# First block of a decoder step: GpSimd's remainders in groups behind DVE's scalings, the memory rows counted by tile, the norm weight spread by TensorE

## The reference

```python
mem_n = rmsnorm(mem_prompt, g_mem[l])                 # 256 memory rows of 1024
mk = mem_n @ w_ck[l];  mv = mem_n @ w_cv[l]           # their keys and values
...
z = rmsnorm(x, g_mix) @ w_in                          # zq, zf, zi, zg, zu, zv, 512 columns each
q = silu(zq); f = lb + (1 - lb) * sigmoid(zf); k = (1 - lb) * sigmoid(-zf); v = zi
S_new, o = hgrn2_scan(S0, q, k, log(f), v)            # recurrence over the tokens, by chunks
o_hg = rmsnorm(o) * hg_norm_g * sigmoid(zg)
o_cm = gelu(zu) * (tril(W_s) @ layernorm(gelu(zv)) + b_s)
x = x + concat(o_hg, o_cm) @ w_out
```

## Time and profile before

| what | us |
|---|---|
| median of 3 runs (2933.69 to 2934.37) | 2933.81 |
| the profiled execution | 2933.21 |
| its span in the trace | 2931.4 |
| PE busy | 2886.1 (98%) |
| DVE busy | 1251.3 (43%) |
| ACT busy | 642.9 (22%) |
| POOL busy | 440.9 (15%) |

### The profile page before, as it was taken

How to read it: one execution, slowest core, us unless ns; L and a number is a source line. 1 busy time by engine, 2 the same in 40 slices (tenths; PEclk the granted TensorE clock), 3 DMA queues, 4 the chain that set the end, 5 groups by cost and what they waited for, 6 DMA issues and landing times.

```text
span 2931.4 us, 40394 instructions
## 1 busy us (share of the span) xinstructions
PE 2886.1 (98%) x17243; PEld 2334.1 (80%) x17243; DVE 1251.3 (43%) x2096; ACT 642.9 (22%) x999; POOL 440.9 (15%) x362
## 2 busy tenths in 40 slices
PE   8998999999999999999999999999999999999998
PEld 7787787777888888788788888877778888877787
DVE  5578443453344733322243744222234473322233
ACT  4435221110123411111122422101012341211011
POOL 0182408788810000000000000000000000000000
PEclk9999999999999999999999999999999999999999
DMA  8895757989975455665666445566767545567654
GB/s 311 311 324 187 278 188 279 361 288 310 329 255 174 154 185 204 222 231 199 223 215 223 142 176 185 199 250 250 274 236 273 178 155 187 180 226 286 235 193 150
DMA packets 207677, 675.93 MB, mean 231 GB/s; under 512 B 22864, under 2 KB 28240, under 8 KB 207504
## 3 DMA queue, kind: packets, MB, share of 16 engines
q1 hardware_dynamic: 200480, 662.72, 63.3%
q10 hardware_dynamic: 7024, 10.68, 1.0%
HBM read 542.84 MB, written 130.48 MB: 230 GB/s over the span
## 4 chain that ended last, share of the span: by engine, by line
PE 89%; DVE 6%; SPq 1%; DMA 1%; ACT 1%; issue 0%; POOL 0%; ACTq 0%; DVEq 0%
PE half L946 81%; PE half L954 2%; PE half L1275 2%; DVE lvl L2238 1%; PE half L1087 1%; PE half L963 1%; DVE lvl L2251 1%; PE half L1155 1%; DMA w_raw<-in_w_out 0%; PE half L1285 0%; DMA mem_raw<-in_w_ck 0%; SPq L599 0%; DMA w_pairs<-stage 0%; DVE state L2287 0%; SPq L779 0%
## 5 line engine op out<-in xcount | busy, mean ns | idle before, releaser
L946 PE MATMUL half<-a_hi,w_ring 128*128 128x512 f32 x2560 | 822.6, 397 | 0.0
L946 PE MATMUL half<-w_ring,a_hi 128*128 128x512 f32 x2176 | 677.1, 392 | 0.0
L946 PE MATMUL half<-w_ring,ht_hi 128*128 128x512 f32 x2016 | 626.5, 392 | 0.0
L946 PEld LDWEIGHTS half<-a_hi,w_ring 128*128 128x128 f32 x2560 | 480.2, 188 | 131.6 <-issue 14.3
L946 PE MATMUL half<-a_lo,w_ring 128*128 128x512 f32 x1280 | 505.4, 395 | 0.0
L946 PEld LDWEIGHTS half<-w_ring,a_hi 128*128 128x128 f32 x2176 | 410.3, 189 | 90.0
L946 PEld LDWEIGHTS half<-w_ring,ht_hi 128*128 128x128 f32 x2016 | 378.9, 188 | 82.2
L946 PE MATMUL half<-w_ring,a_lo 128*128 128x512 f32 x1088 | 433.6, 399 | 5.1 <-DVE a_lo L1839 3.6
L946 PE MATMUL half<-w_ring,ht_lo 128*128 128x512 f32 x1008 | 395.5, 392 | 0.8 <-DVE ht_lo L2464 0.8
L2472 DVE SCALAR_TENSOR_TENSOR x<-half,rstd,x 128x512 f32<-128x512 f32 x252 | 171.7, 744 | 300.7 <-PE half L946 300.7
L946 PEld LDWEIGHTS half<-a_lo,w_ring 128*128 128x128 f32 x1280 | 240.2, 188 | 56.2
(11 more groups left out here) (309 smaller groups left out, 2473.6 us busy)
## 6 DMA issues: line engine op xcount, KB each, us to landing
w_ring<-w_pairs SPq DMA_DIRECT2D x704, 512.0 KB, 3.2
w_pairs<-w_ring SPq DMA_DIRECT2D x192, 512.0 KB, 5.0
w_pairs<-stage SPq DMA_DIRECT2D x16, 1024.0 KB, 6.0
w_raw<-in_w_up SPq DMA_DIRECT2D x64, 256.0 KB, 4.5
w_raw<-in_w_down SPq DMA_DIRECT2D x64, 256.0 KB, 3.9
w_s<-in_w_up SPq DMA_DIRECT2D x8, 2048.0 KB, 11.1
w_s<-in_w_down SPq DMA_DIRECT2D x8, 2048.0 KB, 11.5
w_raw<-in_w_in SPq DMA_DIRECT2D x48, 256.0 KB, 4.3
```

What stands on the lines that cost most here:

```text
L946: m = nc.tensor.matmul(ps[:, j, :], l, r, start=(i == 0 and q == 0), stop=(i == tiles_in - 1 and q == 2))
```

## The change

- `FILLER_HI` has other places for the casts: 33 to 36 behind `kt`, 37 to 39 in unit 0, 40 to 43 in unit 1, 44 and 45 in unit 2, 46 to 48 in unit 3, 49 to 51 in unit 4, 52 to 54 in unit 5, 55 in unit 6.
- GpSimd waits, before the remainders of tiles 29, 33, 37, 40, 44, 46, 49 and 52, for the scalings of units 0 to 7.
- The memory rows come in two loads with a semaphore each; ACT and DVE wait for them by tile.
- The norm weight comes as one row of 4 KB; PE spreads it into PSUM with two products of `ident`'s first element by 512 columns, and DVE's scaling reads it from there.
- Eight products of zeros stand ahead of that, ten more behind the transposes of the rows.
- The gelu table is loaded behind unit 5's `rsqrt`, ahead of the casts.

```diff
-WARM = 20
+WARM = (8, 10)
-FILLER_HI = {"zq": range(29, 33), "kt": range(33, 34), 0: range(34, 38), 1: range(38, 42), 2: range(42, 45), 3: range(45, 47), 4: range(47, 48),
-             5: range(48, 52), 6: range(52, 56)}
+FILLER_HI = {"zq": range(29, 33), "kt": range(33, 37), 0: range(37, 40), 1: range(40, 44), 2: range(44, 46), 3: range(46, 49),
+             4: range(49, 52), 5: range(52, 55), 6: range(55, 56)}
+FILLER_TURN = {29: 0, 33: 1, 37: 2, 40: 3, 44: 4, 46: 5, 49: 6, 52: 7}
...
-            for dst, src in ((x[:, 0:MT, :], I["mem_prompt"][0].rearrange("(t p) d -> p t d", p=P)),
-                             (ident[:], I["c_ident"]), (gain[:], I["g_mem"][0:1, :].broadcast_to([P, D]))):
+            for dst, src in ((gain[0:1, :], I["g_mem"][0:1, :]), (ident[:], I["c_ident"])):
                 sp.dma_start(dst, src).then_inc(mem_in, 16)
+            for t in range(MT):
+                sp.dma_start(x[:, t, :], I["mem_prompt"][0, t * P:t * P + P, :]).then_inc(mem_rows_in[t], 16)
...
             for i in range(first, after):
-
+                if i in FILLER_TURN:
+                    pool.wait_ge(scaled_ready.sem, scaled_ready.at("first", FILLER_TURN[i]))
                 pool.wait_ge(filler_hi, i - first + 1)
...
-            for i in range(WARM):
-                nc.tensor.matmul(half[1][:, 3, 0:P], zero[:].to_broadcast([P, P]), zero[:].to_broadcast([P, P]),
-                                 start=True, stop=True)
-            pe.wait_ge(mem_in, 48)
+            zeros(WARM[0])
+            pe.wait_ge(mem_in, 32)
+            for c in range(2):
+                m = nc.tensor.matmul(half[0][:, 2 + c, :], ident[0:1, 0:1].to_broadcast([1, P]),
+                                     gain[0:1, c * 512:c * 512 + 512], start=True, stop=True)
+            m.then_inc(gain_spread, 1)
             for t in range(MT):
                 pe.wait_ge(xn_ready.sem, xn_ready.at(pos, ("nm", t)))
                 transposes(pos, ("nm", t), [xn[:, t, k * P:k * P + P] for k in range(KD)])
+            zeros(WARM[1])
...
-            act.wait_ge(mem_in, 48)
+            act.wait_ge(mem_rows_in[0], 16)
...
                         rsqrt(pos, "oa", 12)
+                        tables("gelu_apprx_tanh_and_others")
                     filler_tiles(u)
...
-            dve.wait_ge(mem_in, 48)
...
+            dve.wait_ge(gain_spread, 1)
             for t in range(MT):
-                nc.vector.tensor_tensor(xn[:, t, :], x[:, t, :], gain[:], ALU.mult).then_inc(xn_ready.sem, 1)
+                dve.wait_ge(mem_rows_in[t], 16)
+                nc.vector.tensor_tensor(xn[:, t, :].rearrange("p (a c) -> p a c", a=2),
+                                        x[:, t, :].rearrange("p (a c) -> p a c", a=2), half[0][:, 2:4, :], ALU.mult
+                                        ).then_inc(xn_ready.sem, 1)
```

More of the change, by code:

```diff
@@ L378, in program @@
         h0, h1, tl, dn = zip(*(jobs.counts[p] for p in phases))
-        mem_in, consts_in = sem("mem_in"), sem("consts_in")
+        mem_in, consts_in, gain_spread = sem("mem_in"), sem("consts_in"), sem("gain_spread")
+        mem_rows_in = [sem(f"mem_rows_in{t}") for t in range(MT)]
         folded = FOLD1 - FOLD0
@@ L986, in _, with zeros @@
             pe.wait_ge(w_rounded, 1)
-            for i in range(WARM):
-                nc.tensor.matmul(half[1][:, 3, 0:P], zero[:].to_broadcast([P, P]), zero[:].to_broadcast([P, P]),
-                                 start=True, stop=True)
-            pe.wait_ge(mem_in, 48)
+            def zeros(n):
+                for i in range(n):
+                    nc.tensor.matmul(half[1][:, 3, 0:P], zero[:].to_broadcast([P, P]), zero[:].to_broadcast([P, P]),
+                                     start=True, stop=True)
+            zeros(WARM[0])
[4 more added lines that the diff above has]
+            m.then_inc(gain_spread, 1)
             for t in range(MT):
```

## The result

The changed kernel takes 2947.15 us (median of 6 runs, 2945.01 to 2948.18), the one before 2934.64 on the same chip: a ratio of 1.004, with a 95% interval of 1.0029 to 1.0051. The forecast was 2943 us, +9.4; +12.5 was measured. The profiled execution took 2947.42 us (span 2945.6).

The account below looks back on a forecast made before the run. TensorE is busy 2886.1 of 2931.4 us, so only its standstills count. The sum was 2933.2 + 9.4 (later `oto`) + 0 (start) = 2942.6, with 0.6 for the median 2943 us; range 2938 to 2950.

Parts of the forecast that it names:

- Scalings: First block, DVE: unit 3's scalings end 31.4 us after `kt`, at the second block's pace, against 39.1 before.
- the three casts added ahead of unit 0: ACT, first block: 0.6 us each, beside the products of `zv`; taken as nothing, 1.8 us without that cover.
- Loads: First block: remainders 40 to 43 take 5.4 us, load of 47 to load of 48 20.8, landing 14.5.
- Unit 4 to `oto`: First block, PE: 39.7 us, from 36.3 at the second block's pace, 1.9 for `vv` and 1.5 for the clock.
- The clock's price: PE after the standstill at unit 4's products: 1.5 us lost to a lower clock, bounded by 0 and 2.6.
- PE's wait: First block: PE stands still some 22 us before unit 4's products, near 270, for ACT's `gate`.
- The unknown price: Statistics of `vn` beside remainders in unit 2's group: taken as nothing, up to 2 us.
- The start: Kernel start, up to the `kt` transposes: 1.3 us won, up to 1.5 lost on the clock, taken as 0.
- Relief wins: Rival: tile 48's data are there when ACT comes, units 3 to 7 run like the second block's; 2920 us, chance 0.15.
- The load isn't held up: Rival: tile 48 lands 3.4 us after its issue, PE's products start 11.1 us earlier than forecast; 2932 us, chance 0.15.
- The new waits add up: Rival: statistics and remainders collide, clock stays down longer, gelu is held; +17 to +19, 2951 us, chance 0.08.
- The page's rule: First block, remainders 40 to 43: DVE's two-input instructions could make the group 1.4 us longer, sum +10.8; not adopted.

Follow-up runs that it names:

- a_loads: Changed kernel with the sample's 49 small loads and the two zqf loads issued behind the pair loads of tiles 64 to 95; 2930.12 us, ratio 0.9983.
- b_start: Kernel before with the start of the change alone; casts, gelu table and GpSimd as before; 2936.07 us, ratio 1.0002.
- c_split: c_best with vn's scaling split behind the scalings of units 3 and 4, and the lng product behind those of unit 5; 2924.50 us, ratio 0.9961.
- a_zqf: Changed kernel with only the two 2 MB loads of zqf moved, behind the pair loads of tiles 64 to 71; 2937.59 us, ratio 1.0014.
- c_best: a_loads with vn's refinement ahead of unit 3's scalings, vn's scaling behind unit 4's, and tile 54's cast behind unit 6; 2929.48 us, ratio 0.9984.
- b_turns: Kernel before with GpSimd's waits for the scalings of units 0 to 7 alone; casts, start and SP's order unchanged; 2943.81 us, ratio 1.0027.
- b_casts: Kernel before with the new `FILLER_HI` places of the casts alone, without GpSimd's waits for scalings; 2942.54 us, ratio 1.0026.

## Why the prediction was right, step by step

The path named in the forecast is the path of the profile: PE waits once for `gate`, ACT ahead of it for `w_raw<-in_w_out`, ahead of one cast. Its steps, counted from `kt`:

| step | forecast | measured |
|---|---|---|
| end of unit 3's scalings | 31.4 | 247.12 + 2.51 - 216.70 = 32.9 |
| remainders, to the load of 47 | 5.4 | 5.8 |
| load of 47 to load of 48 | 20.8 | 22.0 |
| to the cast of 48 | 14.5 | 13.6 |
| cast, table, sigmoid, to unit 4's outputs | 3.8 | 3.95 |
| unit 4's outputs to `oto` | 39.7 | 336.18 - 294.98 = 41.2 |
| sum | 115.6 | 119.5 |

Five small terms make up the 3.8 us that the stretch took beyond the forecast.

- **Scalings, +1.5.** The subtractions did stand free (2.50 us in each unit). But counted from `kt`, DVE lost time against the second block at two places. The first are the three casts added ahead of unit 0, costed at nothing. Tile 36's cast waited 2.30 us for its load, the gelu of `zv` stands behind it on ACT, PE waited 1.6 us for that (`vn` in the list of waits), and DVE 0.52 us for the `vv` that ACT takes off behind the gelu. I took the casts' time as 0.6 each and left out what they wait for. The second is the instruction for `var` behind the statistics. It took 1.01 us beside the remainders of 37 to 39, and 0.17 in the second block, where GpSimd is quiet:

```profile
232.00 0.61 DVE L2306 SCALAR_TENSOR_TENSOR state<-state,e_last,added 128x128 f32<-128x128 f32 x2 [0.52 <-ACT vv L1673]
...
240.96 1.01 DVE L2367 TENSOR_SCALAR var<-mv 128x4 f32<-128x4 f32 x1
```

```profile
238.14 3.80 POOL L887 TENSOR_TENSOR w_ring<-w_raw,w_ring 128x512 fp32r<-128x512 f32 x3 [7.43 <-DVE lvl L2270]
```

```profile
944.50 0.17 DVE L2348 TENSOR_SCALAR var<-mv 128x4 f32<-128x4 f32 x1
```

  Up to the step on `state` DVE is 15.30 us behind `kt`, in the second block 14.67, so 0.6 of the 1.5 us lie ahead of it; nearly all of the rest is `var`.
- **Loads, +0.4, +1.2 and -0.9.** The issues took 22.0 us this time; over the six profiled kernels with this order of SP it is 20.8 to 23.0, so "nothing in it depends on the engines" holds only to some 2 us.
- **Unit 4 to `oto`, +1.5.** The clock's price, set at 1.5, is right: unit 4's outputs to unit 5's took 307.86 - 294.98 = 12.9 us against 286.41 - 275.15 = 11.3 in a_loads, which did not stand still there (granted clock 0.68 in the first 5 us, against 1.00). The gelu, for which 0 of 0 to 2 was taken, was held: tile 54's cast waited for its load right ahead of it, and `mix` waited 1.7 us, where the later blocks wait 0.5:

```profile
317.26 0.62 ACT L1688 CAST w_ring<-w_raw 128x512 fp32r<-128x512 f32 x1 [1.24 <-DMA w_raw<-in_w_out]
317.79 1.87 ACT L1723 ACTIVATE uu<-half 128x2048 f32<-128x2048 f32 x1
```

- **PE's wait, 16.6 and not some 22.** PE came to the standstill at 278.4, not near 270: it had lost 4.8 us at unit 3 and 1.6 behind the gelu of `zv`. Both were paid for by the standstill, so the time does not show them.
- **The unknown price** was sought at the wrong instructions. The statistics took 2.46 us beside remainders, as without them. But `var` right behind them lost 0.84 us on the path, and the refinement and the scaling that follow, not named in the forecast either, took 4.1 us more than in the second block. These were hidden here; they are what a_loads still pays.
- **The start, 0,** is right (b_start), but partly by luck. Eight zeros took 3.64 us and not 2.9, and the products that spread the weight 1.98 and not 2.9; the errors cancel, and DVE's first scaling began at 6.81 (forecast 7.0). PE's wait for the fourth group is 0.6 to 4.1 us in the profiled kernels that have this start, forecast 2.8. But its load was to land 1.3 us earlier; the cast that waits for it starts on average 0.2 us earlier (six kernels at 31.0, four with the old start at 31.2), and in the profiled execution of the changed kernel 2.5 later:

```profile
33.91 1.90 ACT L1504 CAST w_ring<-mem_raw 128x2048 fp32r<-128x2048 f32 x1 [11.35 <-DMA mem_raw<-in_w_ck]
```

  In that execution SP's issues of `lbp` took 4.03 us (2.4 to 2.9 in the others); why was not tried. The clock did stay at its upper level from 14 to 20 us.
- **A reading.** Of the 4.3 us in four waits that the forecast puts into the first block's units, two waits with 3.8 us lie there. No term of the sum uses them.

**The rivals.** "Relief wins" was priced at 2920. Where the relief was really given, in a_loads, it won 6.0 us on the stretch and not 14, since the second block's pace was taken for DVE although the remainders had only moved, from beside `lvl` to beside `vn`; only c_split comes near (a stretch of 95.9 us, where 92.3 were reckoned). "The load isn't held up" fell to the profile (13.6 us), and a_zqf shows what it would have meant: 2937.6, not the 2932 given for it. "The new waits add up" named the held gelu rightly, but there was 1.2 us of it.

**The page's rule** (the Trainium skill, "SBUF — State Buffer", "Who interferes with whom") said that a group of remainders and DVE's two-input instructions lock each other out for whole instructions. By the forecast's estimate that would have made the group 1.4 us longer. The group took 5.23 us, against 5.04 of the first group of four, which had no DVE instruction beside it: 0.2 us longer, and not 1.4. But the subtractions that the estimate counted no longer stood beside it, only two of the short instructions of the refinement; so the estimate was not put to the test as it was worked out. Other rows show just what the rule describes: each of these two instructions of 128x4 took 1.2 to 1.3 us beside remainders, about one remainder's 1.26, and two remainders took 4.5 us about DVE's one long product with `lng` (2.28 us; 2 x 1.26 + 2.28 = 4.8). The same section counts `tensor_scalar` in its two-port modes among the instructions that contend, and with that half of the rule the scaling of `vn` (3.84 against 1.92 us) and `var` (1.01 against 0.17) would have been on the forecast's list; the forecast weighed only the two-input half. That they run in such a mode is not shown by itself here.

## What to carry to other kernels

Before a use is moved ahead on an in-order engine, follow its data back through every queue: here the wait of one cast held a sigmoid, and this a whole half of PSUM, while the load stood behind 49 small issues and 4 MB that nobody needed for another 200 us (`zqf`'s first product begins at 508.6). And work that is moved from beside one instruction stands beside another: look at what is there before the relief is booked.

## What was not expected

- DVE beside GpSimd: statistics (128x512) 2.46 us against 2.45, `copy_predicated` unchanged, but instructions of 128x4 1.0 to 1.3 us against 0.16, and a `tensor_scalar` of four times 128x512 3.84 against 1.92. In these rows the size does not tell what the neighbour costs.
- The clock fell in the changed start, ahead of the place that was watched. Behind the two one-row products and a wait of 1.31 us the 16 transposes took 3.58 us (2.18 before), and the granted clock of 8 to 10 us (seventh column) was 0.51:

```profile
4.80 1.98 PE L1001 MATMUL half<-gain,ident 1*128 1x512 f32 x4
8.09 3.58 PE L958 MATMUL half<-ident,xn 128*128 128x128 f32 x16 [1.31 <-DVE xn L1965]
```

```profile
8.00:10.00 2.00, 1.91 (x9) 1.91 (x10) 1.17 (x2) 0.00 (x0) 0.00 (x0) 0.51 1.02 385
...
12.00:14.00 2.00, 1.90 (x17) 1.71 (x16) 2.00 (x3) 2.00 (x3) 0.00 (x0) 1.00 1.05 388
```

  Which of the two made it fall was not tried. It cost nothing here: with the ten zeros that follow the clock was up again from 12 us, and the first key product began at 14.81, as before. The start is not the same in every execution, though. In the seven profiles that have it the transposes took 3.3 to 3.7 us; in two of them (a_loads, c_best) the one-row products took 3.78 us as well, and the first key product began only at 16.7. Even so `kt` began earliest in these two, at 214.7 and 214.2.
- Each half of the change loses about 8 us alone (b_turns +8.7, b_casts +7.4) and both lose 12.5: they do not add up. Both traces show the same load at work: one half asks for it later, the other needs it earlier.
